# Delta rule's norms and gates inside attention's stage, GpSimd's level masks there too, and the modulation gates summed and spread in another way

## The chip, the cores and the metric

One core of one Trainium2 chip runs the whole kernel in one launch. The metric is the device time of that launch in microseconds (us), the median of several runs. TensorE multiplies matrices into PSUM, VectorE and ScalarE do element-wise work, GpSimd builds masks and does some element-wise work, and SyncE issues most of the transfers.

## What is computed

Two transformer layers over 256 tokens of width 1,024, in f32. The change lies in the first layer:

```python
mod = jax.nn.silu(c) @ w_ada + b_ada
shift1, scale1, gate1, shift2, scale2, gate2 = [m[:, None, :] for m in jnp.split(mod, 6, axis=-1)]
h = modulate(rms_norm(x, norm1_gain), shift1, scale1)
proj = h @ w_in
o_a = chunked_band_attention(qa, ka, va, attn_q_gain, attn_k_gain, attn_rel_bias)   # 8 heads of 64
o_a = rms_norm(o_a, attn_out_gain)
qkv_b = causal_depthwise_conv(qkv_b, dn_conv_w)
q_b = l2_norm(q_b); k_b = l2_norm(k_b)                                              # 4 heads of 128
beta = jax.nn.sigmoid(b_raw)
g = -jnp.exp(dn_a_log) * jax.nn.softplus(a_raw + dn_dt_bias)
o_b = gated_delta_rule(q_b, k_b, v_b, g, beta)                                      # chunks of 128
o_b = rms_norm(o_b, dn_out_gain) * jax.nn.silu(z_b)
x = x + gate1 * (jnp.concatenate([o_a, o_b], axis=-1) @ w_out)
h2 = modulate(rms_norm(x, norm2_gain), shift2, scale2)
x = x + gate2 * peer(h2, ...)
```

Within a chunk the delta rule needs the cumulated gates gc, the decays exp(gc_i - gc_j) below and above the diagonal, the Gram products k k^T and q k^T, and the inverse of a unit lower triangular matrix.

## The kernel before, in words

The program is a row of stages (`nc.Block`). At the end of each, all engines meet at a barrier. Within a stage each engine has its instructions in a fixed order, written out by hand, and waits on semaphores for the others. Nothing reorders them.

1. **First projection** (L637). c goes through SiLU and is kept as the same row on all 128 partitions (`c_row`). The first norm and the product with w_in run while the weights stream through a ring of four 1 MB slots. The modulation vector has 48 blocks of 128 outputs. Each takes one tile of w_ada, 128 x 1024, which VectorE multiplies with `c_row` and sums along the row (L752 for the first 16 tiles, `fill_mods` at L439 for the other 32). The tiles of `fill_mods` pass through five buffers, `fill_tiles`; `load_fills` (L430) lets SyncE load a tile once the sum before it in that buffer is done.
2. **Attention's stage** (L943). TensorE turns q and k (four banks), adds the bias and forms scores for two halves of four heads. VectorE takes the maxima (L970), ScalarE the exponentials (L1014), TensorE turns the probabilities in six banks, VectorE and ScalarE copy three each, TensorE forms the heads (L1079). Then come the row norm of the result (L989, L1026, L996) and, for the delta rule, the sums of squares of q and k as 16 products with one column (L1086). Between these, VectorE runs the last three taps of v's convolution (`add_tap`, L731) and nine tile sums. With gate 1's eight sums done, GpSimd stores the gate's column to HBM (`store_gate`, L447) and later loads it as a row on all partitions (`load_gate`, L453).
3. **Preparation of the delta rule** (L1122). VectorE spreads the inverse norms (L1178), TensorE turns them (L1239), VectorE scales q and k (L1200). The gate g is formed from a_raw by small operations on both engines, cumulated by TensorE (L1244), then come differences (L1206 to L1209), exponentials (L1166 to L1169), masks and beta (L1214 to L1217), the Gram products (L1251) and their scaling (L1221 to L1224), the transposes of k and v (L1255), and the scaled copies kbg, kdec and vb (L1231 to L1233). GpSimd writes six level masks meanwhile (`level_masks`, L1123).
4. **Inverse and delta rule** (L1275). Six doubling levels of 64 x 64 blocks: TensorE forms X (L1315), ScalarE copies it (L1365), TensorE forms the updates (L1320, L1321; all through `blocks`, L1301), VectorE subtracts them (L1395, L1397) and then does two tile sums. Products with u, w and the state, the output norm and the gating follow (L1412 to L1430).
5. **w_out** (`rows_stage`, L1433), the query stage (L1559), and the **experts' stage** (L1706), whose up half adds gate 2 times its result to x (L1972). Tile sums stand beside w_out's products and in the query stage; gate 2 goes through HBM like gate 1, at the start of the experts' stage (L1710).

The time of an f32 product lies in its passes: the profile counts two MATMUL rows for each. In the listings of the instructions one row stands for one product.

## Time and profile before

| | |
|---|---|
| Median of three runs | 1701.43 us (1698.95 to 1707.26) |
| The profiled execution | 1696.9 us, its span 1695.2 us, mean granted clock 0.973 |
| TensorE busy | 1582.3 us (93%) |
| VectorE busy | 1239.3 us (73%) |
| ScalarE busy | 899.9 us (53%) |
| GpSimd busy | 45.0 us (3%) |
| Moved by transfers | 314.37 MB, 185 GB/s on the mean |

Busy shares are means over very different stages, so a stage is read from its own window, and inside it from the order in time: which engine starts late, and who released it. The clock is the share of TensorE's 2.4 GHz that was granted; it stands at 1.0 or at 0.5 (1.2 GHz), and values between are stretches with a change inside.

### The profile page before, as it was taken

The numbers are of one execution on the slowest core, as the hardware profiler recorded it, in microseconds if no ns is written. First come the engines' busy times: TensorE is split into PE (matmuls) and PEld (weight loads), VectorE is DVE, ScalarE is ACT, GpSimd is POOL, SyncE is SP. The second block draws the span as 40 slices with busy tenths as digits, with TensorE's granted clock in tenths as the row PEclk, the third lists the DMA queues.
The fourth block names the chain that finished last, engine by engine and source line by source line (L and its number), as shares of the span: only waits on it lengthen the run. The fifth ranks groups of instructions, "written<-read, shape, count | busy, mean of one in ns | idle before, by whom it ended". The sixth has DMA issues, their size and how long they took to land. (4 is left out here: it accounts for less than half of the span.)

```text
span 1695.2 us, 26555 instructions
## 1 busy us (share of the span) xinstructions
PE 1582.3 (93%) x10358; PEld 1430.0 (84%) x10358; DVE 1239.3 (73%) x2494; ACT 899.9 (53%) x1497; POOL 45.0 (3%) x83
## 2 busy tenths in 40 slices
PE   5986779899999999999999999999999889889998
PEld 5975668899999999988888888797888777789997
DVE  5887777688997999957677666657787566654564
ACT  6763255555545555545555555456555756455453
POOL 0002300000000000000000000020000000000000
PEclk9997889999999999999999999989999899999999
DMA  9953446476666545557666666644444223345552
GB/s 325 342 173 103 151 168 195 119 238 229 227 224 212 162 149 163 153 205 252 238 244 239 246 239 238 243 143 157 144 140 139 75 75 123 132 151 191 176 195 102
DMA packets 110808, 314.37 MB, mean 185 GB/s; under 512 B 8464, under 2 KB 9056, under 8 KB 101216
## 3 DMA queue, kind: packets, MB, share of 16 engines
q1 hardware_dynamic: 98976, 276.94, 48.4%
q10 hardware_dynamic: 11040, 33.66, 5.5%
q0 software_dynamic: 672, 2.12, 0.4%
q8 instruction: 82, 1.34, 0.3%
q14 instruction: 38, 0.31, 0.1%
HBM read 293.80 MB, written 18.89 MB: 184 GB/s over the span
## 5 line engine op out<-in xcount | busy, mean ns | idle before, releaser
L300 PE MATMUL ps<-parts,parts 128*128 128x512 f32 (+1 forms) x4992 | 970.9, 356 | 20.9 <-DVE parts L290 15.1
L300 PEld LDWEIGHTS ps<-parts,parts 128*128 128x128 f32 x4992 | 823.4, 191 | 156.7 <-DVE parts L290 15.9
L285 ACT CAST parts<-lead 128x512 fp32r<-128x512 f32 x940 | 579.8, 621 | 618.2 <-PE ps L300 395.1
L290 DVE TENSOR_TENSOR parts<-lead,parts 128x512 fp32r<-128x512 f32 x940 | 640.7, 688 | 336.1 <-ACT parts L285 333.0
L1743 PE MATMUL ps<-parts,parts 128*128 128x256 f32 x3072 | 385.3, 285 | 4.5 <-DVE parts L290 4.5
L1743 PEld LDWEIGHTS ps<-parts,parts 128*128 128x128 f32 x3072 | 372.6, 192 | 5.5 <-DVE parts L290 5.5
L376 PE MATMUL ps<-lead,mem 128*128 128x128 f32 (+2 forms) x292 | 45.9, 321 | 51.0 <-ACT mem L492 26.4
L376 PEld LDWEIGHTS ps<-lead,mem 128*128 128x128 f32 (+2 forms) x292 | 40.3, 160 | 56.7 <-ACT mem L492 27.9
L1917 DVE TENSOR_SCALAR mem<-lead,mem 128x128 f32<-128x128 f32 x256 | 70.9, 338 | 0.0
L1729 PE MATMUL ps<-mem 128*128 128x128 f32 x512 | 67.8, 275 | 0.7 <-DVE mem L1917 0.7
L1729 PEld LDWEIGHTS ps<-mem 128*128 128x128 f32 x512 | 62.8, 192 | 1.1 <-issue 1.1
L1914 DVE TENSOR_SCALAR mem<-lead,mem 128x128 f32<-128x128 f32 x256 | 55.4, 278 | 0.0
L1947 DVE TENSOR_TENSOR mem<-mem 128x1024 f32<-128x1024 f32 x32 | 39.0, 1219 | 5.9 <-DMA mem<-act_spill 5.9
L1952 DVE TENSOR_TENSOR parts<-mem,parts 128x1024 fp32r<-128x1024 f32 x32 | 39.0, 1218 | 0.0
L1800 ACT CAST parts<-mem 128x1024 fp32r<-128x1024 f32 x32 | 33.4, 1045 | 9.1 <-DVE mem L1947 7.9
L1804 ACT COPY mem<-ps 128x512 f32<-128x512 f32 x64 | 37.0, 579 | 0.0
L1301 PE MATMUL ps<-mem 64*64 64x64 f32 x512 | 19.7, 238 | 17.7 <-POOL mem L1287 14.8
L444 DVE SCALAR_TENSOR_TENSOR mem<-mem 128x1024 f32<-128x1024 f32 x27 | 34.8, 1308 | 0.1
L1301 PEld LDWEIGHTS ps<-mem 64*64 64x64 f32 x512 | 18.3, 151 | 19.2 <-POOL mem L1287 16.1
L1783 ACT ACTIVATE mem<-ps 128x1024 f32<-128x1024 f32 x32 | 32.6, 1020 | 0.0
L2096 PEld LDWEIGHTS ps<-mem 128*128 128x128 f32 x256 | 29.8, 192 | 0.6
L2096 PE MATMUL ps<-mem 128*128 128x128 f32 x256 | 29.9, 275 | 0.0
(339 smaller groups left out, 972.8 us busy)
## 6 DMA issues: line engine op xcount, KB each, us to landing
...
act_spill<-mem ACTq DMA_DIRECT2D x32, 512.0 KB, 5.5
mem<-act_spill ACTq DMA_DIRECT2D x32, 512.0 KB, 3.3
mem<-in_w_ada SPq DMA_DIRECT2D x27, 512.0 KB, 5.3
...
```

The source lines that it names most:

```text
L285: act.copy(w_hi[g % BUFFERS], st.words(n, u * UNIT, UNIT)).then_inc(hi_ready, 1)
L290: dve.tensor_tensor(w_lo[g % BUFFERS], st.words(n, u * UNIT, UNIT), w_hi[g % BUFFERS].bitcast(F32), ALU.subtract).then_inc(lo_ready, 1)
L300: mm = pe.matmul(o, lhs[a], rhs[b], start=start and i == 0, stop=stop and i == 2, skip_group_check=True, **kw)
L376: last = pe.transpose(o, i, ident[0:i.shape[0], 0:i.shape[0]])
L1301: mm = pe.matmul(ps[rows, bank, u % 4 * HP:(u % 4 + 1) * HP], left[rows, :], right[rows, :], start=True, stop=True)
L1729: mm = pe.matmul(ps[:, 4 + b % 4, j * P:(j + 1) * P], one1[b % 2][:, j, :], one2[b % 2][:, j, :], start=True, stop=True)
L1743: mm = pe.matmul(ps[:, c % 2 * 2 + m // 2, m % 2 * S:(m % 2 + 1) * S], parts[a][:, ms], (x_hi, x_lo)[b][:, k, :], start=k == 0 and i == 0 ...
L1914: one = dve.tensor_scalar(one1[b % 2][:, j, :], iota, pick(0, b * GT + j), None, ALU.is_equal)
L1917: one = dve.tensor_scalar(one2[b % 2][:, j, :], iota, pick(1, b * GT + j), pick(2, b * GT + j), ALU.is_equal, ALU.mult)
L1947: dve.tensor_tensor(got[q % 2], got[q % 2], at(O_R + q * 1024, 1024), ALU.mult).then_inc(s_pr, 1)
L1952: dve.tensor_tensor(a_lo[q], got[q % 2], a_hi[q].bitcast(F32), ALU.subtract).then_inc(s_al, 1)
L2096: mm = pe.matmul(psf[:, 2048 + u * P:2048 + (u + 1) * P], k, q, start=True, stop=True)
```

## The change

- **Gate 1 on TensorE.** The eight tiles of gate 1 are stored on the host with the input index on partitions. c is turned in the first stage (eight transposes, one copy into `c_wide`, 64 equal columns for each of eight blocks). TensorE sums the gate over eight tiles as 16 products of 64 x 512, one half of the tile to PSUM partitions 0 to 63, the other to 64 to 127 of one bank (`gate_sums`), at the end of the preparation, behind the Grams. ScalarE copies the bank at that stage's end. At the end of the next stage four products with a single row of ones spread it (and its bias) over all partitions, and ScalarE copies it to `gate1`. Gate 1 no longer goes through HBM.
- **Order and buffers of the tiles.** Seven buffers instead of five. VectorE sums two tiles in attention's stage instead of nine, none instead of three in the preparation, eleven instead of thirteen in the inverse's stage, three instead of four beside w_out. Gate 2's eight tiles are loaded and summed in the up half, one every eight units (`load_late`, `late_mod`); its column is turned by TensorE before the store.
- **Moved to attention's stage:** the gate g and beta (beta by exp and reciprocal, not Sigmoid), the sums of squares of q and k (now four 512-column products with a matrix of ones, which give the sums spread over all partitions), their roots as exp(-0.5 ln), the scaling of q and k, the cumulated gates, and GpSimd's level masks. Scores lie in three banks per half instead of four, and VectorE copies all six banks of turned probabilities.
- **Preparation:** GpSimd masks the upper decay matrix with a select; ScalarE forms kbg and kdec from PSUM and does v's SiLU at the end. v is turned and scaled in the next stage.

```diff
-        FILL1, FILL2, FILL3, FILL4 = 9, 12, 25, 32
+        order = [KT, KT + 1] + list(range(KT)) + list(range(KT + 2, 3 * KT))
+        PE_SUMS = (2, KT + 2)
+        TAIL_SUMS = 21
...
+        def gate_sums(pe):
+            for p in range(*PE_SUMS):
+                k = order[p]
+                pe.wait_ge(s_fill[p % FILLS], 16 * (p // FILLS + 1))
+                for h in range(2):
+                    mm = pe.matmul(ps[h * 64:(h + 1) * 64, 7, :], c_wide[:, k, :],
+                                   fill_tiles[p % FILLS][:, h * 512:(h + 1) * 512], start=k == 0, stop=k == KT - 1)
+                mm.then_inc(s_mod, 1)
+        def load_late(sp, i):
+            sp.dma_start(late_tiles[i], A["w_ada"][(5 * KT + i) // 2][:, i % 2 * D:(i % 2 + 1) * D]).then_inc(s_late, 16)
...
@@ attention's stage, VectorE
+                dve.wait_ge(s_par_dn, 48)
+                step(dve.tensor_tensor(by_tile(gc_), ab[:, :, 1, :], dn_par[:, 4:8].unsqueeze(1).to_broadcast([P, TT, HD]), ALU.add))
+                step(dve.tensor_scalar(tmp_, gc_, -1.0, None, ALU.mult))
+                dve.tensor_tensor(tmp_, tmp_, gc_, ALU.max).then_inc(s_gpre, 1)
                 add_tap(dve, vstep, 2, 1)
-                fill_mods(dve, 0, 2)
+                fill_mods(dve, 0, PE_SUMS[0])
...
-                    fill_mods(dve, 2 + 2 * half, 4 + 2 * half)
-                for b in range(0, 6, 2):
+                for b in range(6):
...
+                for i in range(2):
+                    v = conv[:, 4 * i:4 * i + 4, :].rearrange("p a t -> p (a t)")
+                    dve.wait_ge(s_root, i + 1)
+                    dve.scalar_tensor_tensor(out=v, in0=v, scalar=1.0 if i else P ** -0.5, in1=qk_roots[:, i, :],
+                                             op0=ALU.mult, op1=ALU.mult)
+                dve.wait_ge(s_gcm, 1)
+                dve.tensor_copy(gcB, psf[:, 2560:3584].rearrange("p (u t) -> p u t", t=P))
@@ attention's stage, ScalarE, between and behind the exponentials
+                    if half == 0:
+                        act.wait_ge(s_silu, 1)
+                        act.activation(at(O_H, 8 * S), conv[:, 0:8, :].rearrange("p a t -> p (a t)"), ACT.Square).then_inc(s_sq, 1)
+                act.wait_ge(s_ge, 1)
+                act.activation(tmp_, tmp_, ACT.Ln, bias=1.0).then_inc(s_gl, 1)
+                for i in range(2):
+                    act.wait_ge(s_ssum, i + 1)
+                    act.activation(qk_roots[:, i, :], psf[:, 3072:4096], ACT.Ln, bias=eps).then_inc(s_ln, 1)
+                for i in range(2):
+                    act.wait_ge(s_ln, i + 1)
+                    act.activation(qk_roots[:, i, :], qk_roots[:, i, :], ACT.Exp, scale=-0.5).then_inc(s_root, 1)
@@ attention's stage, TensorE
+                    if b == 3:
+                        pe.wait_ge(s_sq, 1)
+                        square_sums(0)
...
+                    if hd == 4:
+                        pe.wait_ge(s_ln, 1)
+                        square_sums(1)
@@ preparation, GpSimd and ScalarE
-                level_masks(pool, lev, 6, s_lv, False)
+                pool.wait_ge(s_dexp, 2)
+                pool.affine_select(out=DT, in_=DT, compare_op=ALU.is_ge, fill=0.0, base=0, pattern=[[0, U], [1, P]],
+                                   channel_multiplier=-1).then_inc(s_upper, 1)
...
+                for u in range(U):
+                    act.activation(kbg[:, u, :], kt[:, u, :], ACT.Identity, scale=beg_[:, u:u + 1])
...
+                act.activation(conv[:, 8:12, :], conv[:, 8:12, :], ACT.Silu)
+                act.wait_ge(s_mod, PE_SUMS[1])
+                act.copy(gate_row, ps[:, 7, :])
@@ inverse, VectorE, per level, and TensorE at the end
-                    fill_mods(dve, FILL2 + 2 * i, FILL2 + 2 * i + 2)
+                    fill_mods(dve, PE_SUMS[1] + i, PE_SUMS[1] + i + 1)
...
+                fill_mods(dve, PE_SUMS[1] + 9, TAIL_SUMS)
                 dve.wait_ge(s_o, 1)
...
+                for h in range(2):
+                    pe.matmul(ps[:, h, :], ones[h * 64:h * 64 + 1, :], gate_row[h * 64:h * 64 + 1, :], start=True, stop=False)
+                for h in range(2):
+                    mm = pe.matmul(ps[:, h, :], ones[h * 64:h * 64 + 1, :], gate_bias[h * 64:h * 64 + 1, :], start=False, stop=True)
+                mm.then_inc(s_gb, 1)
@@ up half, SyncE and VectorE
+                st.issue(sp, n_up[0] + 24)
+                sp.wait_ge(s_pr, 12)
+                for i in range(KT):
+                    load_late(sp, i)
+                    st.issue(sp, n_up[0] + 26 + 2 * i)
...
+                    if i % 8 == 7 and 20 <= q < 20 + KT:
+                        late_mod(dve, q - 20)
```

How the instructions stand, at the two places of which the prediction speaks. First TensorE in the preparation, before (between the jumps of the two stages; L1239 spreads the norms, L1242 and L1244 cumulate the gates, L1251 are the Grams, L376 transposes):

```order
L1239 MATMUL ps<-lead,mem 128x128 x16
L1242 MATMUL ps<-mem,lead 128x8
L1244 MATMUL ps<-lead,mem 128x128 x8
L1251 MATMUL ps<-mem 128x128 x16
L376 MATMUL ps<-lead,mem 128x128 x16
```

and TensorE in the same stage of the changed kernel, with the first row of the next stage (L1300 are the Grams, L459 the sums of gate 1):

```order
L1300 MATMUL ps<-mem 128x128 x16
L376 MATMUL ps<-lead,mem 128x128 x8
L459 MATMUL ps<-mem 64x512 x8
L459 MATMUL ps<-lead,mem 64x512 x2
L459 MATMUL ps<-mem 64x512 x6
L1231 UNCONDITIONAL_BRANCH
L1343 UNCONDITIONAL_BRANCH
L376 MATMUL ps<-lead,mem 128x128 x8
```

The spreading of the norms and the cumulation went ahead into attention's stage, v's eight transposes behind the stage's end, and the sixteen products of the gate came in.

Second, VectorE from the start of attention's stage to the second maxima, before (L961 takes q and k out, L731 are taps, L444 tile sums, L970 the maxima):

```order
L961 TENSOR_SCALAR mem<-ps,lead 128x512 x2
L731 SCALAR_TENSOR_TENSOR mem<-mem,lead 128x256 x4
L444 SCALAR_TENSOR_TENSOR mem,lead<-mem 128x1024 x2
L970 TENSOR_REDUCE lead<-ps 128x4 x2
L974 TENSOR_SCALAR lead<-lead 128x2x4
L731 SCALAR_TENSOR_TENSOR mem<-mem,lead 128x256 x4
L444 SCALAR_TENSOR_TENSOR mem,lead<-mem 128x1024 x2
L970 TENSOR_REDUCE lead<-ps 128x4 x2
```

and in the changed kernel (L1033 takes q and k out, L1036 to L1038 the gate's sum, L765 taps, L449 tile sums, L1048 maxima):

```order
L1033 TENSOR_SCALAR mem<-ps,lead 128x512 x2
L1036 TENSOR_TENSOR lead<-mem,lead 128x8
L1037 TENSOR_SCALAR lead<-lead 128x8
L1038 TENSOR_TENSOR lead<-lead 128x8
L765 SCALAR_TENSOR_TENSOR mem<-mem,lead 128x256 x4
L449 SCALAR_TENSOR_TENSOR mem,lead<-mem,lead 128x1024 x2
L1048 TENSOR_REDUCE lead<-ps 128x4 x2
L1051 TENSOR_SCALAR lead<-lead 128x2x4
L765 SCALAR_TENSOR_TENSOR mem<-mem,lead 128x256 x4
L1048 TENSOR_REDUCE lead<-ps 128x4 x2
```

Three small operations stand ahead of the first tap, and the two tile sums between the maxima are gone.

## Rows read from the trace of the kernel before

**Rows 1.** Windows, whole kernel: stretch, us, then busy (instructions) of each engine, clock, DMA share, GB/s

```profile
107.50:141.20 33.70, 25.60 (x200) 24.06 (x200) 25.90 (x48) 20.01 (x50) 0.92 (x2) 0.87 0.51 159
141.20:172.10 30.90, 14.34 (x98) 13.91 (x98) 24.92 (x39) 10.99 (x15) 10.40 (x25) 0.72 0.21 68
172.10:214.80 42.70, 31.49 (x608) 29.34 (x608) 31.41 (x69) 11.13 (x35) 13.76 (x8) 0.86 0.46 150
...
760.00:1085.00 325.00, 324.76 (x1432) 268.43 (x1432) 229.89 (x302) 174.48 (x271) 0.00 (x0) 1.00 0.69 245
```

**Rows 2.** DMA issues by line: KB each, median us from issue to landing

```profile
mem<-in_w_ada SPq DMA_DIRECT2D x27, 512.0 KB, 5.3
...
lead<-in_dn_out_gain SPq DMA_DIRECT2D x1, 64.0 KB, 4.3
...
gate_rows<-lead POOLq DMA_DIRECT2D x2, 4.0 KB, 10.3
```

**Rows 3.** Order in time, attention's stage: start us, duration us, engine, line, operation

```profile
108.34 0.43 SPq L948 DMA_DIRECT2D lead<-in_dn_out_gain  x1
...
109.73 1.66 DVE L731 SCALAR_TENSOR_TENSOR mem<-mem,lead 128x256 f32<-128x256 f32 x4
...
113.80 1.82 DVE L970 TENSOR_REDUCE lead<-ps 128x4 f32<-128x512 f32 x2
...
115.86 0.37 ACT L1014 ACTIVATE mem<-ps,lead 128x128 f32<-128x128 f32 x1 [0.21 <-DVE lead L974]
...
121.78 0.37 ACT L1014 ACTIVATE mem<-ps,lead 128x128 f32<-128x128 f32 x1 [2.60 <-DVE lead L974]
...
124.96 1.95 ACT L1018 ACTIVATE mem<-mem 128x2048 f32<-128x2048 f32 x1
...
127.53 6.20 PE L1079 MATMUL ps<-mem 128*128 128x64 f32 x48
...
136.58 1.28 ACT L1029 ACT_TABLE_LOAD   x1
137.87 0.29 ACT L1029 ACTIVATE lead<-lead 128x2 f32<-128x2 f32 x1
...
138.40 1.54 DVE L996 SCALAR_TENSOR_TENSOR mem<-mem,lead 128x512 f32<-128x512 f32 x2
```

**Rows 4.** Order in time, preparation of the delta rule: TensorE, GpSimd, VectorE

```profile
143.25 6.75 PE L1239 MATMUL ps<-lead,mem 128*128 128x128 f32 x32 [4.74 <-DVE mem L1178]
...
151.36 0.51 POOL L1148 COPY mem<-mem 64x384 f32<-64x384 f32 x1
...
153.02 3.84 PE L1251 MATMUL ps<-mem 128*128 128x128 f32 x32 [1.01 <-DVE mem L1200]
...
159.90 1.22 DVE L1214 TENSOR_TENSOR mem<-mem,lead 128x1024 f32<-128x1024 f32 x1 [1.54 <-ACT mem L1169]
...
170.17 1.21 DVE L1233 TENSOR_TENSOR mem<-ps,mem 128x1024 f32<-128x1024 f32 x1
```

**Rows 5.** Order in time, inverse and delta rule

```profile
180.67 0.28 DVE L1395 TENSOR_TENSOR mem<-mem,ps 128x128 f32<-128x128 f32 x1
...
185.68 3.12 PEld L1301 LDWEIGHTS ps<-mem 64*64 64x64 f32 x96 [1.31 <-issue]
...
195.62 0.28 DVE L1395 TENSOR_TENSOR mem<-mem,ps 128x128 f32<-128x128 f32 x1
...
196.60 1.14 PE L1325 MATMUL ps<-mem 64*64 64x64 f32 x16 [0.59 <-DVE mem L1397]
...
206.85 0.69 DVE L1417 COPY mem<-ps 128x512 f32<-128x512 f32 x1 [1.62 <-PE ps L1344]
```

**Rows 6.** Windows of TensorE alone: stretch, us, busy (instructions), clock, DMA share, GB/s

```profile
145.00:147.50 2.50, 2.50 (x14) 0.50 0.55 120
...
177.50:180.00 2.50, 2.50 (x48) 0.50 0.17 49
...
215.00:217.50 2.50, 2.50 (x13) 0.50 0.00 0
```

444 lines of the change are left out of this document (233 added, 211 removed).

## Prediction, made before the changed kernel was run

> **What bounds the kernel now.** I read the windows of each stage first, then the waits and the order in time inside the three stages that the change rewrites, and last the landing times of the transfers. The windows [rows 1] show four of the stretches: attention's stage 107.5 to 141.2 us, the preparation of the delta rule 141.2 to 172.1, the inverse and the delta rule 172.1 to 214.8, and the up half of the experts' stage. Behind the third TensorE is busy nearly all the time (324.8 of 325.0 us in the up half), so only added waits could be felt there. In the first three no engine is full: 25.6, 14.3 and 31.5 us of TensorE, 25.9, 24.9 and 31.4 of VectorE. They are chains of small steps that hand work from engine to engine, with a barrier at each end. The preparation is the thinnest: 30.9 us, mostly one VectorE chain, which ends with six multiplications between 160 and 171.4 [rows 4] while TensorE does nothing.
>
> **Attention's stage: longer by 5.0.** (1) VectorE now computes the gate's sum behind its first two evacuations, and that waits for all three delta parameters. The last of them is issued at 108.34 [rows 3] and lands 4.3 later [rows 2], at 112.6. The gate's three small operations take about 0.8, so the first tap begins at 113.5, where it began at 109.73 [rows 3]. The two gate-tile sums behind it stay, so the first maximum starts at 117.6, not 113.80, and the first exponentials at 119.7, not 115.86. (2) Each half of the exponentials takes 3.3 [rows 3]. ScalarE's square of 1.95 moves between the halves. The second half so ends at 119.7 + 3.3 + 1.95 + 3.3 = 128.3; it ended when the square began, at 124.96: + 3.3. VectorE is not late for it, since the two gate-tile sums of 1.2 between the maxima are gone. (3) From there to the last head was 8.7 us (to 127.53 + 6.20 [rows 3]). Now TensorE adds the second pair of sums of squares between the heads. They are two 512-column products in f32; 128 columns cost 3.84 / 32 = 0.12 a pass [rows 4], two passes each, so four times that comes to 1.9 for both. VectorE copies all six transposed banks; three take 1.9 and are early. The heads end at 138.5, which is 4.8 later. (4) Behind the heads stood 6.2 us, to the end of the last row at 138.40 + 1.54 [rows 3]. Now: two evacuations 1.3, two normalisations of q and k of 1.22, the copy of the cumulated gates 1.2, small ones 0.4, the two rows 1.5, in sum 6.8. The stage ends at 145.3 and the barrier's 1.2 follow: 146.2 to 146.5 against 141.2, so **+5.0** (3 to 8: three if the parameters land after 2.5 us as the earlier two did, eight if TensorE, idle for 4.7 us before the transposes, runs them and the heads at half clock). Hidden there: GpSimd's masks, 10.7 us from the stage's start to 151.9 [rows 4], which nothing needs before the inverse.
>
> ScalarE's table changes in this stage go from three to five. A change costs 1.28 in the rows, and the next operation starts 0.01 behind it (136.58 + 1.28, then 137.87 [rows 3]). The two new ones run beside TensorE's heads, so I cost them at nothing; without that cover they cost 2.6. The Trainium skill, "ScalarE: Activation LUTs", What ACT_TABLE_LOAD costs, puts a drain of about 1.38 us to each change, some 2.66 in all. By that this stage would be 2.8 longer still. The trace disagrees, since its rows leave no room for a drain.
>
> **The preparation: shorter by 12.7.** Spreading of norms, gates, cumulated sums and the scalings of k and v leave VectorE. Its new chain is ten operations of 0.7 to 1.2 and two short waits, about 12 us, with GpSimd's select (128 x 64 elements take 0.3 to 1.5, so 128 x 1024 about 2) beside it. ScalarE's chain, with 12 scalings of about 0.3, two table changes and the SiLU of v, ends near 14. The longest is now TensorE's, because the gate's eight sums are queued behind the Grams, and ScalarE waits for them at the stage's end. Its terms from the start: 16 Gram products at the clock that TensorE has after idling, 6.8 (the first 32 passes of this stage took 6.75 with 0.50 granted [rows 4, 6]); 8 transposes 1.0; then 16 products of 64 x 512, 32 passes of 4 x 0.12 less their tails, 14.4 us if one runs after the other. But the two halves of a tile go to different column halves of the array. For such pairs the nearest rows are the 64 x 64 blocks of the inverse, which differ in rows and columns: 96 passes in 3.12, 0.033 each, where unpaired ones need 1.14 / 16 = 0.071 [rows 5]. That is an overlap by two or more; a pair that shares its rows may do less. I take a factor of 1.6: 8.9 us, between 7.2 and 14.4. With ScalarE's copy of 0.6, the barrier's 0.7 and 0.2 of hand-over: 6.8 + 1.0 + 8.9 + 1.5 = 18.2 against 30.9, so **-12.7** (-14.4 to -7.2). The last gate tile is loaded once the first sum is done and lands 5.3 later [rows 2], about 14 us in, before its turn. The bias is fetched by 1,024 elements of 4 bytes, as the store of the gate was, which took 10.3 [rows 2]; it is wanted only in the next stage.
>
> The Trainium skill, "TensorE: Matmul & The Clock Gate", Why this matters for your kernels, says that products with few output columns overlap if each goes to its own column group, 2.38 times for three of them. By that two halves would come close to full overlap, 7.5 us, and the sum would be 1.4 lower. No row of the trace before has such a pair.
>
> **Inverse and w_out: shorter by 4.1.** VectorE's gate-tile sums go from two to one per level. The updates begin at 180.67 and then every 3.7 us on the mean until 195.62 [rows 5]. TensorE alone needs 3.1 a level for its 96 passes plus a hand-over, 3.3, so four intervals give 1.6 back. The first level runs at half clock now (0.50 until 180 us). Behind the sums TensorE is warm, and with one sum less the second update comes 2.4 earlier. The scaling of v by ScalarE (0.7 a level) and its transposes (1.0) fit into waits. At the end two sums stand between the copies and the first output rows, which are ready at 206.85 [rows 5]: +0.5; the broadcast of the gate by four products and two ScalarE copies ends 0.1 behind the old end: +0.6 in all. It also keeps TensorE busy up to w_out's transposes, which now run at 0.50 [rows 6]: -0.7. Sum: -1.6 - 2.4 + 0.6 - 0.7 = **-4.1** (-6 to -1).
>
> **Elsewhere: nothing.** In the first stage the transposes and the copy of c fall into VectorE's and TensorE's waits before 21 us. The last eight tiles are loaded and summed in the up half: 1.3 us of VectorE every 10.9, where it is idle 95 of 325 us [rows 1], and 47 GB/s on top of 245 with the transfer engines busy 0.69. If that cover is gone, a stall of 1 us per tile costs 8.
>
> **Sum.** +5.0 - 12.7 - 4.1 = -11.8. The profiled execution took 1696.9 us, so 1685.1. The median of the runs stands 4.5 above it, at 1701.4; I add half of that and predict **1687.5**.
>
> **Rivals.** *The halves don't overlap.* The preparation is then only 7.2 shorter, the sum -6.3, the time 1693. For it: they read the same rows and no row shows such a pair; against it: the 64 x 64 pairs do overlap. *Attention's stage grows by 10* (half clock, the roots on the path): -6.8, 1692.5. For it: the clock was 0.50 in the preparation [rows 6] after 4.7 us without work [rows 4], and the new gaps are about as long. *The sums bind the stage and slow the kernel:* if TensorE stays at half clock through the preparation and the halves don't overlap, the sums take 28.8, the stage 6.8 + 2 + 28.8 + 1.5 = 39, which is 8 longer; with +5.0 and about -3 behind it: +10, 1709. It decides once the sums take longer than 24 us. For it: in the inverse TensorE stayed at 0.50 for 6 us of work; against it: 512-column products keep it far busier, and it reached full clock within 7 us in each stage. *It doesn't do what it says:* the masks were done at 151.9 [rows 4] while the stage lasted to 172, so moving them is worth nothing by itself; that is in my sum already.
>
> **How the numbers follow.** A run of this kernel tells 0.5% (8.5 us) from no change. Forecast (-8.5 to -18) 0.60; no overlap 0.18; long attention 0.12; the sums at half clock 0.07; 0.03 for full overlap and everything hidden, below the range. The range takes the forecast's bounds, the two middle cases and part of the last: 1679 to 1700. Faster 0.63, same 0.30, slower 0.07.
>
> **What would show it.** Right: the preparation lasts about 18 us and its last wait is ScalarE's for the gate's sums, which run in 8 to 10 us; attention's stage lasts 38 to 39 with the first maximum near 117.6; TensorE is at full clock at the inverse's first level and at w_out's start; the up half stays at 325. Wrong: sums of 14 us or more, a first maximum near 114, or new waits for transfers in the up half.

## The result, and the profile after

The changed kernel ran in a median of **1680.01 us** (1679.39 to 1681.05, four runs) against 1700.38 us before (1698.95 to 1707.26, four runs): a ratio of 0.9873, 95% interval 0.9856 to 0.9889. It is faster by 20.4 us, or 1.1 to 1.4%: under 2%, but clear of the noise, since the interval leaves out 1. Its profiled execution took 1681.05 us, with a span of 1679.3 us, so span against span the change gives 15.9 us. I had predicted 1685.1 for the profiled execution and 1687.5 for the median: the right direction, inside the range of 1679 to 1700, and too slow by 7.5 us. The 15.9 lies within the forecast's own bounds (8.5 to 18 less), the medians' 20.4 beyond them.

First the windows of the changed kernel, cut at its own stage starts, with the up half last (columns as in [rows 1]):

```profile
107.74:142.93 35.19, 27.18 (x194) 23.32 (x194) 25.08 (x49) 25.36 (x55) 9.73 (x23) 0.92 0.16 48
142.93:157.66 14.73, 13.77 (x73) 8.77 (x73) 10.54 (x14) 10.24 (x21) 1.64 (x2) 0.85 0.39 115
157.66:198.50 40.84, 31.81 (x624) 28.51 (x625) 27.66 (x62) 14.19 (x45) 11.96 (x8) 0.96 0.46 154
744.00:1069.00 325.00, 324.96 (x1435) 268.65 (x1434) 238.94 (x320) 174.84 (x270) 1.15 (x2) 1.00 0.75 258
```

With the stage starts of the kernel before read to the hundredth (107.53, 141.17, 172.06, 214.88), the stages compare so (the 0.7 us that the prediction gave to w_out's start falls into the row below the inverse's):

| us | before | predicted | after | step was off by |
|---|---|---|---|---|
| attention's stage | 33.64 | +5.0 | 35.19 (+1.6) | -3.4 |
| preparation | 30.89 | -12.7 | 14.73 (-16.2) | -3.5 |
| inverse's stage, w_out | 42.82 | -4.1 | 40.84 (-2.0) | +2.1 |
| all else, up half included | | 0 | +0.7 | +0.7 |
| sum | | -11.8 | -15.9 | -4.1 |

A stage's start is here the first operation of any engine behind the barrier. Before the change that was GpSimd's at 172.06, 0.4 us behind the barrier; cut at the barrier's end, the preparation gave 15.8 and the inverse 2.4.

The windows of the up half were both chosen 325 us long, so they compare its rate and not its length: TensorE is busy for 324.96 us with 1,435 rows of products, against 1,432 before [rows 1], with VectorE 9 us busier and the transfers at 0.75 instead of 0.69. VectorE waits there for transfers (of `act_spill`) five times, 3.4 us in all, against once and 0.2 before. These are the new waits that the prediction named as a sign of being wrong, but TensorE doesn't feel them. With all behind the inverse at 1480.8 us against 1480.3, the cover held.

**Attention's stage** of the changed kernel, order in time (the rows that answer to [rows 3]):

```profile
112.64 0.17 DVE L1036 TENSOR_TENSOR lead<-mem,lead 128x8 f32<-128x8 f32 x1 [2.60 <-DMA lead<-in_dn_out_gain]
...
113.16 1.68 DVE L765 SCALAR_TENSOR_TENSOR mem<-mem,lead 128x256 f32<-128x256 f32 x4
...
117.20 1.81 DVE L1048 TENSOR_REDUCE lead<-ps 128x4 f32<-128x512 f32 x2
...
122.43 1.95 ACT L1114 ACTIVATE mem<-mem 128x2048 f32<-128x2048 f32 x1
...
127.64 1.53 PE L376 MATMUL ps<-lead,mem 128*128 128x128 f32 x12
...
129.01 2.79 PE L1201 MATMUL ps<-mem 128*128 128x64 f32 x24
...
131.64 1.94 PE L1167 MATMUL ps<-mem,lead 128*128 128x512 f32 x4
...
133.41 2.79 PE L1201 MATMUL ps<-mem 128*128 128x64 f32 x24
...
136.31 1.29 DVE L1071 TENSOR_TENSOR mem<-ps,lead 128x512 f32<-128x512 f32 x2 [4.26 <-PE ps L1201]
...
141.25 1.41 DVE L1085 SCALAR_TENSOR_TENSOR mem<-mem,lead 128x512 f32<-128x512 f32 x2
```

The predicted wait is there: VectorE stands 2.60 us for the last of the parameters, and the first maximum starts at 117.20 (predicted 117.6). The heads take 2 x 2.79 = 5.6 us where they took 6.2, and the last row ends at 142.66, only 0.27 ahead of the next stage.

**The preparation** of the changed kernel, order in time (against [rows 4]):

```profile
142.97 5.87 PE L1300 MATMUL ps<-mem 128*128 128x128 f32 x32 [4.71 <-PEq L1011]
...
147.89 1.12 POOL L1245 TENSOR_SCALAR_AFFINE_SELECT mem<-mem 128x1024 f32<-128x1024 f32 x1 [4.45 <-ACT mem L1254]
...
149.64 3.65 PE L459 MATMUL ps<-mem 128*64 128x512 f32 x16
...
153.13 1.03 PE L459 MATMUL ps<-lead,mem 128*64 128x512 f32 x4
...
153.55 1.22 DVE L1292 TENSOR_TENSOR mem<-ps,mem 128x1024 f32<-128x1024 f32 x1
...
153.99 2.74 PE L459 MATMUL ps<-mem 128*64 128x512 f32 x12
...
156.78 0.58 ACT L1266 COPY mem<-ps 128x512 f32<-128x512 f32 x1 [1.47 <-PE ps L459]
...
157.66 1.06 PE L376 MATMUL ps<-lead,mem 128*128 128x128 f32 x8 [0.93 <-PEq L1231]
```

As predicted the stage ends in ScalarE's wait for the gate's sums. These take 7.1 us (149.64 to 156.73), not 8.9. VectorE is done at 154.77.

**The inverse**, order in time (against [rows 5]), and TensorE's windows alone (against [rows 6]):

```profile
164.06 0.28 DVE L1463 TENSOR_TENSOR mem<-mem,ps 128x128 f32<-128x128 f32 x1
...
166.79 4.32 PE L1349 MATMUL ps<-mem 64*64 64x64 f32 x128 [0.35 <-issue]
...
172.64 7.06 PE L1349 MATMUL ps<-mem 64*64 64x64 f32 x211 [1.52 <-issue]
...
178.81 0.29 DVE L1463 TENSOR_TENSOR mem<-mem,ps 128x128 f32<-128x128 f32 x1 [0.57 <-PE ps L1349]
...
198.50 3.59 PE L376 MATMUL ps<-lead,mem 128*128 128x128 f32 x16 [2.38 <-PEq L1323]
```

```profile
145.00:147.50 2.50, 2.50 (x15) 0.54 0.20 1
...
185.00:187.50 2.50, 2.50 (x14) 0.50 0.41 164
...
200.00:202.50 2.50, 2.50 (x14) 0.62 0.00 0
```

The second update starts 6.40 us after the stage's start (164.06 - 157.66) where it started 8.61 after it (180.67 - 172.06). But the next four intervals take 14.75 us, hardly less than the 14.95 before: in the third, at the fourth level, TensorE stands for 1.52 us with no releaser ("issue"). At the start of w_out the clock is again at half (0.50 from 198.5 to 201.9).

### The profile page after: what moved, and what is told of

It is laid out like the page before. It is cut to its first block and busy times, and to the rows that moved or that the text cites. A ratio compares the mean times of both kernels' runs of the same rounds, so it can differ in the third digit from the quotient of the medians.

```text
span 1679.3 us, 26490 instructions
## 1 busy us (share of the span) xinstructions
PE 1586.3 (94%) x10351; PEld 1426.4 (85%) x10351; DVE 1226.5 (73%) x2476; ACT 907.7 (54%) x1519; POOL 42.7 (3%) x82
## 5 line engine op out<-in xcount | busy, mean ns | idle before, releaser
L376 PE MATMUL ps<-lead,mem 128*128 128x128 f32 (+2 forms) x292 | 45.5, 319 | 44.9 <-ACT mem L519 23.4
L376 PEld LDWEIGHTS ps<-lead,mem 128*128 128x128 f32 (+2 forms) x292 | 39.8, 159 | 52.6 <-ACT mem L519 24.8
L786 DVE SCALAR_TENSOR_TENSOR lead<-lead 128x1024 f32<-128x1024 f32 x16 | 18.9, 1218 | 2.1 <-DMA lead<-in_w_ada 2.1
```

The source lines that it names most:

```text
L376: last = pe.transpose(o, i, ident[0:i.shape[0], 0:i.shape[0]])
```

## Experiments

Fifteen more runs were made, one of them the changed kernel unedited. What each left in its profiled execution is gathered here (us). Most were executed once, so the verdicts rest on the stages and not on the times. The changed kernel's own two rows show how far a stage moves with no edit at all: 1.7 us in attention's stage, 0.4 in the preparation, 1.0 in the inverse.

| kernel | whole | attention | preparation | inverse | all behind it | TensorE's waits for "issue" in the inverse |
|---|---|---|---|---|---|---|
| before | 1696.9 | 33.64 | 30.89 | 42.82 | 1480.3 | 0.37 |
| square between (before) | 1696.8 | 33.96 | 30.90 | 42.27 | 1480.2 | none |
| store later (before) | 1700.6 | 32.84 | 30.94 | 46.00 | 1480.4 | none so named |
| changed | 1681.1 | 35.19 | 14.73 | 40.84 | 1480.8 | 0.35, 1.52 |
| changed, again | 1682.8 | 36.89 | 15.13 | 39.89 | 1481.6 | 0.65, 1.25 |
| same columns | 1694.1 | 36.58 | 21.85 | 39.04 | 1486.9 | none |
| no sums | 1681.2 | 36.54 | 13.32 | 42.09 | 1480.8 | none |
| gate later | 1678.1 | 32.79 | 14.98 | 39.85 | 1482.3 | 0.37, 1.52 |
| parts early | 1679.2 | 35.25 | 14.33 | 40.03 | 1480.3 | 1.06, 0.15 |
| both | 1684.5 | 32.95 | 15.74 | 39.50 | 1486.8 | 1.25, 0.37 |
| scaling in preparation | 1687.2 | 36.06 | 17.14 | 43.70 | 1480.8 | 0.47, 1.52 |
| masks in preparation | 1690.7 | 36.61 | 15.18 | 42.05 | 1487.4 | 0.32, 1.24 |
| upper on VectorE | 1679.9 | 36.33 | 15.03 | 40.63 | 1478.2 | 0.46, 1.52 |
| short loads | 1681.1 | 35.21 | 14.08 | 39.65 | 1481.3 | none |
| short loads, two sums | 1684.1 | 35.61 | 14.13 | 43.48 | 1481.4 | none |
| loads held | 1686.7 | 36.60 | 15.00 | 39.11 | 1485.7 | none |
| gate later, loads held | 1680.0 | 32.72 | 15.55 | 39.67 | 1482.6 | 0.21 |

The spread of attention's stage goes with TensorE's clock. In the three kernels with the gate later the granted clock is 1.00 from 115 to 137 us, and the stage lasts 32.7 to 33.0. In the other versions of the changed kernel it falls to 0.50 around the first transposes of the probabilities: for 3.4 us where the stage lasts 35.2 to 36.1 (the changed kernel's first profile, from 123.4 to 126.8), for 6.8 where it lasts 36.3 to 36.9 (its second, from 122.3 to 129.1).

### Do the column halves overlap?

```diff
-                    mm = pe.matmul(ps[h * 64:(h + 1) * 64, 7, :], c_wide[:, k, :],
+                    mm = pe.matmul(ps[0:64, 7 - h, :], c_wide[:, k, :],
```

> The changed kernel, with both halves of each gate tile sent to the same 64 output columns of TensorE (PSUM partitions 0 to 63 of two banks). The second half of gate 1 is therefore not the reference's. In the changed kernel the 32 passes take 7.1 us and the preparation lasts 14.7. Theory: this is so because the two halves run beside each other, and the sums are what the preparation ends with. Then the sums take 14.2 us here (32 x 0.44), the preparation 21.8, and the time is about 7 us longer, 1688. Rival: a pass with 64 output columns is simply short (0.22 us), whatever its neighbour does. Then the sums stay at 7.1 us and the preparation at 14.7.

Order in time of TensorE, of this kernel:

```profile
151.54 7.08 PE L459 MATMUL ps<-mem 128*64 128x512 f32 x16
158.46 1.88 PE L459 MATMUL ps<-lead,mem 128*64 128x512 f32 x4
160.18 5.31 PE L459 MATMUL ps<-mem 128*64 128x512 f32 x12
```

The 32 passes take 13.95 us (151.54 to 165.49) instead of 7.1, and the preparation 21.85 instead of 14.73. The expectation came true in both places, and the overlap is a factor of 1.97, practically full. The time rose by 13 us, not by 7. The other 6 lie behind the inverse (1486.9 against 1480.8) and come again in kernels whose results are the reference's (both, masks in preparation), so nothing ties them to this edit. About 5 of the 6 can be placed: in all three of these kernels the granted clock is 0.50 for 10.2 us near 1380 (1385.1 to 1395.3 here) with TensorE busy throughout, where the changed kernel has 1.00; half of that time is 5.1.

### What bounds the preparation next, and does TensorE stay warm?

```diff
-                    mm = pe.matmul(ps[h * 64:(h + 1) * 64, 7, :], c_wide[:, k, :],
-                                   fill_tiles[p % FILLS][:, h * 512:(h + 1) * 512], ...)
+                    mm = pe.matmul(ps[h * 64:(h + 1) * 64, 7, 0:8], c_wide[:, k, :],
+                                   fill_tiles[p % FILLS][:, h * 512:h * 512 + 8], ...)
```

> The changed kernel with each of the gate's products cut from 512 to 8 columns, so that gate 1 is not computed and TensorE does nearly nothing behind the transposes of the preparation. Theory: the sums hide all but their last 1.4 us behind ScalarE's chain, so the preparation ends with ScalarE's SiLU of v and lasts 13.2 us instead of 14.7; and, as my prediction priced it, they keep TensorE warm, so that without them the first level of the inverse runs at half clock and the inverse's stage is about 2.4 us longer than 40.8. Rival: the inverse's first level is bound by GpSimd's and VectorE's hand-overs, not by the clock; then the preparation is 1.5 shorter and the inverse stays within 0.5 us of 40.8.

The preparation lasts 13.32 us and ends, as expected, behind ScalarE's SiLU of v, which has no wait behind it any more. So sums worth 7.1 us cost 1.4. The inverse is 1.25 us longer than the changed kernel's although it has no stop. Its second update starts 8.63 us after the stage's start (6.40 there): 2.2 us, close to the 2.4 that the prediction gave to the warm clock and one sum less together. The granted clock, which with the sums is 1.00 from 147.3 to 184.8, is 0.50 here from 154.8 to 165.1. The four intervals behind it take 12.56 us.

### ScalarE's square between the halves

```diff
 @@ before: attention's stage, ScalarE
                     one.then_inc(s_exp, 1)
+                    if half == 0:
+                        act.wait_ge(s_silu, 1)
+                        act.activation(at(O_H, 8 * S), ..., ACT.Square).then_inc(s_sq, 1)
-                act.wait_ge(s_silu, 1)
-                act.activation(at(O_H, 8 * S), ..., ACT.Square).then_inc(s_sq, 1)
                 for b in range(1, 6, 2):
```

> The kernel before, with ScalarE's Square of 1.95 us moved from behind the second half of the exponentials to between the halves; all else as before. My prediction added the full 1.95 us to attention's stage for this move. By that pricing the stage goes from 33.7 us to 35.6. Rival: in the kernel before the square stood ahead of ScalarE's three copies of the turned probabilities, and the heads waited for those; moved, it costs 1.95 in one place and gives it back in the other, and the stage stays at 33.7 within 0.4.

Order in time of ScalarE and TensorE, of this kernel:

```profile
119.20 1.95 ACT L1019 ACTIVATE mem<-mem 128x2048 f32<-128x2048 f32 x1
...
121.94 0.37 ACT L1014 ACTIVATE mem<-ps,lead 128x128 f32<-128x128 f32 x1 [0.80 <-DVE lead L974]
...
125.33 2.66 PE L376 MATMUL ps<-lead,mem 128*128 128x128 f32 x12 [4.40 <-ACT mem L1014]
...
127.78 6.03 PE L1080 MATMUL ps<-mem 128*128 128x64 f32 x48
```

The stage is 0.3 us longer, so the result is the rival's, but its reason is not. The second half of the exponentials starts when it did, at 14.3 us from the stage's start, because ScalarE had waited 2.60 us there for the second maxima [rows 3]. The square fills that wait and leaves 0.80 of it. A gap is worth as much as the work that is put into it. In the changed kernel this wait is gone, as the two tile sums between the maxima are, and ScalarE goes through the first half, the square and the second half without a stop (119.25 to 127.59). There the square does cost its 1.95, as the prediction had it.

### Who holds the barrier of attention's stage?

```diff
 @@ before, GpSimd: attention's stage, preparation
-                store_gate(pool, 0, 2)
+                pass
...
+                store_gate(pool, 0, 2)
                 level_masks(pool, lev, 6, s_lv, False)
```

> The kernel before, with GpSimd's store of gate 1 to HBM moved from attention's stage to the start of the preparation; all else as before. The last VectorE row of attention's stage ended at 139.94 us and the next stage began at 141.17, which is 1.23 later; in the changed kernel the gap is 0.27. Theory: GpSimd reaches the barrier only when its store of 10.3 us has landed (issued 130.66, so 140.96), and this sets the end of the stage. Then the gap is 0.3 here and attention's stage is 0.9 shorter, 32.8 us, while the preparation stays at 30.9. Rival: the gap is the barrier's own cost; then it stays at 1.2 and nothing changes.

VectorE at the stage's end, of this kernel:

```profile
139.55 1.54 DVE L996 SCALAR_TENSOR_TENSOR mem<-mem,lead 128x512 f32<-128x512 f32 x2
141.63 0.25 DVE L1177 RECIPROCAL lead<-lead 128x16 f32<-128x16 f32 x1 [0.54 <-PEq L943]
```

The gap is 0.54 us where it was 1.26, and attention's stage 32.84 where it was 33.64. GpSimd's store, which takes 10.3 us to land [rows 2], held the barrier: before, it landed at 140.85 and GpSimd reached the barrier at 140.97. The time as a whole doesn't show the gain. In this one execution the inverse took 46.00 us instead of 42.82, with a tile sum beside GpSimd of 2.33 instead of 1.31 and the clock at 0.50 once more from 187.9 to 191.3. The change removes it with gate 1's way through HBM. I had carried the 1.2 over as the barrier's own cost.

### The parameters' wait

```diff
 @@ changed kernel: attention's stage, VectorE (the three small operations with their wait)
-                dve.wait_ge(s_par_dn, 48) ... .then_inc(s_gpre, 1)
                 add_tap(dve, vstep, 2, 1)
-                fill_mods(dve, 0, PE_SUMS[0])
+                fill_mods(dve, 0, 1)
+                dve.wait_ge(s_par_dn, 48) ... .then_inc(s_gpre, 1)
+                fill_mods(dve, 1, PE_SUMS[0])
```

> The changed kernel, with the gate's three small VectorE operations (which wait for the delta rule's parameters) moved from ahead of v's tap to between the two tile sums; nothing left out. Attention's stage lasted 35.2 us in the changed kernel's profile and 36.5 in two of its variants that changed nothing there; VectorE waited 2.6 to 3.2 us for the parameters, and where it waited longer TensorE turned the first probabilities in 2.8 us, not 2.1. Theory: the wait is on the stage's path, so the first maximum comes at 7.0 us from the stage's start and not at 9.5, and the stage lasts 32 to 33 us. Rival: behind the wait something else is late (TensorE's products, ScalarE's two SiLUs, which end 8.7 us from the start), and no more than 1 us is gained.

VectorE and TensorE, of this kernel, whose stage starts at 106.48:

```profile
111.89 0.17 DVE L1038 TENSOR_TENSOR lead<-mem,lead 128x8 f32<-128x8 f32 x1 [0.27 <-DMA lead<-in_dn_out_gain]
...
113.53 1.81 DVE L1049 TENSOR_REDUCE lead<-ps 128x4 f32<-128x512 f32 x2
```

```profile
118.97 1.53 PE L376 MATMUL ps<-lead,mem 128*128 128x128 f32 x12 [0.88 <-ACT mem L1110]
```

The first maximum comes 7.05 us from the start, and the stage lasts 32.79 us. That is 2.4 below the changed kernel's profile and 4.1 below its second one. The second part is the clock: where VectorE comes late, TensorE has been idle for 4.05 us and turns the first probabilities at half clock, 2.82 us against 1.53 above. This row is of the changed kernel run again:

```profile
123.14 2.82 PE L376 MATMUL ps<-lead,mem 128*128 128x128 f32 x12 [4.05 <-ACT mem L1109]
```

### Scalings and masks, back in the preparation

```diff
 @@ preparation, VectorE and TensorE (and out of attention's stage)
+                for i in range(2):
+                    ... dve.scalar_tensor_tensor(out=v, in0=v, ..., in1=qk_roots[:, i, :]).then_inc(s_qkn, 1)
+                pe.wait_ge(s_qkn, 2)
```

> The changed kernel, with VectorE's two scalings of q and k by their inverse norms (2.35 us) moved back to the start of the preparation, the Grams waiting for them; nothing left out. Theory: in attention's stage they stand beside ScalarE's squares, table load and root for the row norm, so taking them out gives back 1.0 to 1.2 us of it, while the preparation becomes longer by the full 2.4 us, since the Grams and the sums behind them are its path: +1.3 in sum, 17.1 us for the preparation. By my prediction's pricing (all 2.4 us on attention's path, and the preparation bound by TensorE) the two cancel and the sum is 0. Third possibility: TensorE, idle for longer ahead of the Grams, stays at half clock for longer, and the preparation is more than 3 us longer.

```profile
137.25 1.29 DVE L1071 TENSOR_TENSOR mem<-ps,lead 128x512 f32<-128x512 f32 x2 [4.26 <-PE ps L1196]
...
141.66 0.29 ACT L1124 ACTIVATE lead<-lead 128x2 f32<-128x2 f32 x1
```

The preparation is longer by 2.4 us against the changed kernel's profile and by 2.0 against its second one, about the 2.35 of the scalings. In attention's stage the way from VectorE's first evacuation of the heads to the next stage is 6.62 us (137.25 to 143.87), and it is 6.62 in the changed kernel too (136.31 to 142.93). The move gives nothing back there. ScalarE's roots, squares, table load and square root bind that end, and VectorE's scalings lie beside them. ScalarE's squares could start when VectorE's evacuations end at 137.60 in the changed kernel, and they start at 137.95, when the roots are done; so the roots and their table change cost 0.35 us there and not nothing. My theory's gain of 1.0 to 1.2 was wrong, and so was the prediction, which had put VectorE's 6.8 us on the path and found nearly the right length with the wrong engine. The inverse of this execution, 43.70, has the stop of 1.52 again and then the clock at 0.50 from 177.9 to 181.3, which the changed kernel doesn't have.

```diff
 @@ GpSimd: level masks out of attention's stage, ahead of the select in the preparation
-                pool.wait_ge(s_tr, 4)
-                level_masks(pool, lev, 6, s_lv, False)
...
+                level_masks(pool, lev, 6, s_lv, False)
                 pool.memset(TI_all[HP:P, :, 0:HP], 0.0).then_inc(s_zero, 1)
```

> The changed kernel, with GpSimd's level masks (10.7 us) moved back to the start of the preparation, ahead of its select of the upper decay matrix; nothing left out. Theory: in attention's stage nothing waits for the masks, and in the preparation they delay the select to about 153.7 us and VectorE's last product to about 156, still before TensorE's sums end at 156.7: both stages stay as they are, within 0.3 us. Rival: GpSimd's masks beside VectorE's chain slow it (in the inverse a tile sum beside GpSimd took 2.08 us, not 1.22), so that VectorE ends behind TensorE and the preparation is 1 to 3 us longer, while attention's stage, freed of the masks, is shorter by up to 1 us.

```profile
155.73 1.34 POOL L1245 TENSOR_SCALAR_AFFINE_SELECT mem<-mem 128x1024 f32<-128x1024 f32 x1
...
156.04 1.31 DVE L1288 COPY mem<-mem 128x512 f32<-128x512 f32 x1
...
157.98 1.23 DVE L1292 TENSOR_TENSOR mem<-ps,mem 128x1024 f32<-128x1024 f32 x1
```

The preparation is 15.18 us (15.13 and 15.00 in two executions with the masks in attention's stage), so the masks' place is worth nothing that can be told. It is close, though. The select comes 11.4 us after the stage's start, the copy of 0.43 us takes 1.31 beside it, and VectorE's last product ends 0.3 ahead of the next stage, together with ScalarE's copy. With the masks here, TensorE and VectorE bind the stage alike. Attention's stage did not gain by their absence (36.61).

```diff
 @@ preparation: select on GpSimd -> product on VectorE
-                pool.affine_select(out=DT, in_=DT, ...).then_inc(s_upper, 1)
+                dve.tensor_tensor(DT, DT, upper.unsqueeze(1).to_broadcast([P, U, P]), ALU.mult).then_inc(s_upper, 1)
```

> The changed kernel, with the upper decay matrix masked by a VectorE product with the 0/1 matrix (1.22 us), as in the kernel before, and not by GpSimd's select; nothing left out. Theory: VectorE ended at 154.8 us in the changed kernel, 1.9 ahead of TensorE's sums at 156.7, so 1.2 more still lie beside them and the preparation stays at 14.7 us within 0.3. Rival: in that case the wait for the select was VectorE's own slack, and with the product inside its chain the first parts of L come later; then the preparation is still the same but VectorE ends less than 1 us ahead. It would be worth 1 us or more only if VectorE were the bound.

The preparation lasts 15.03 us, inside the spread of the unedited one, and the time is 1679.91. VectorE ends at 156.52, 1.7 us ahead of TensorE's sums. The GpSimd select is worth nothing here while these end the stage.

### The inverse: VectorE's sums, GpSimd's parts, TensorE's stop

> The changed kernel, with 32 of the 1,024 columns of each of the last fourteen tiles of w_ada loaded in the preparation and the inverse (the same number of transfers, 16 KB each for 512 KB), so that shift and scale 2 are not the reference's. In the inverse of the changed kernel TensorE stood still for 1.5 us after no semaphore at 171.1, while one 16 KB packet of its instructions had arrived at 170 behind tile transfers that filled the queues; the kernel before had such an interval too, and in two variants of the changed kernel the five levels took 3.14 us each without it. Theory: TensorE's instructions come late behind the tiles. Then there is no such stop here, the updates follow each other every 3.1 us and the inverse lasts 38.7 us instead of 40.8. Rival: the stop has nothing to do with the tiles and comes in about every second execution; then this run shows it or not, and the level intervals that contain an instruction packet are long as well.

```diff
+                wide_ = D if p < PE_SUMS[1] else 32
-                sp.dma_start(fill_tiles[p % FILLS], A["w_ada"][j][:, half * D:(half + 1) * D])
+                sp.dma_start(fill_tiles[p % FILLS][:, 0:wide_], A["w_ada"][j][:, half * D:half * D + wide_])
```

TensorE in the levels, of this kernel, which is one unbroken row of 15.14 us:

```profile
162.98 15.14 PE L1350 MATMUL ps<-mem 64*64 64x64 f32 x464 [0.50 <-DVE mem L1466]
```

The stop is gone, and the second to sixth updates start at 164.86, 167.82, 170.96, 174.09 and 177.23, so 12.37 us for four intervals instead of 14.75. The inverse lasts 39.65 us, not 38.7. From the last first-half update to w_out it takes 20.9 us against 19.7, with the clock lower there. That end differs by up to 2.5 us between executions of all versions.

> The changed kernel, with SyncE's last seven tile loads held until VectorE has summed the tile of the fifth level; nothing left out. In the changed kernel they start at 163 us, and TensorE stops at 171.1 for 1.5 us. With short loads (one thirty-second of the bytes) the stop was gone and the levels took 3.14 us each. Theory: it is the tile bytes that keep TensorE's instructions waiting; held back, they leave the fourth level free, the five updates follow each other every 3.1 us, and the inverse is 1.5 to 2.2 us shorter than 40.8, unless the sums at its end now wait for their tiles. Rival: the short loads removed the stop through the tiles loaded in the preparation, not through these seven; then it stays.

```diff
+                sp.wait_ge(s_mod, PE_SUMS[1] + 5)
                 load_fills(sp, PE_SUMS[1] + FILLS, 3 * KT)
```

```profile
164.68 11.51 PE L1350 MATMUL ps<-mem 64*64 64x64 f32 x350 [0.50 <-DVE mem L1466]
```

With all results kept, holding back seven tiles removes the stop as well: four intervals take 12.46 us, and the inverse 39.11 (39.89 in the changed kernel beside it). The changed kernel's second execution shows the stop once more, at the same level (1.25 us). So it follows from the tile transfers, and not from the last seven alone: it is absent too in same columns, where the first two of these seven are issued at the same times from the stage's start (6.5 and 8.8 us), but the eight tiles before them over 12.0 us instead of 6.0 (150.76 to 156.77 in the changed kernel).

That it is TensorE's instructions which come late behind them shows in where the stops stand. Count the MATMUL rows of the whole kernel, starting with 0. The nine executions with such waits have 17 of them in the inverse, and each stands just ahead of row 978 (979 in parts early and both), row 1106 or row 1234. These are 128 rows apart, whatever the level and whatever the engines beside TensorE do; the x128 between the waits of 0.35 and 1.52 above is one such stretch. The instructions arrive in packets of 16 KB, about one for each stretch. In the six executions with the long stop ahead of row 1106, the packet that precedes it begins 3.3 to 3.6 us after row 978 has started; in same columns, no sums, short loads, held loads and the last version below, which have no stop there, it begins 0.6 to 1.6 us after it. At every one of the 17 stops TensorE goes on 1.25 to 1.51 us after a packet has ended: in the changed kernel the packet ends at 171.38 and row 1106 starts at 172.64. So the instructions come late, and with the tile loads taken away they don't; the queue in which the packets wait isn't seen.

> The kernel with the short loads, and with two tile sums behind each level of the inverse (as before the change) instead of one, and none further on in that stage; shift and scale 2 are not the reference's. My prediction priced the second sum at 0.4 us a level (1.6 for four intervals). By that the interval between updates is 3.5 to 3.7 us here. Rival: TensorE's 96 products and two hand-overs make the interval, a second sum of 1.15 us fits behind the updates, and the interval is 3.1 to 3.3 us, so that what the change saved in the levels was not VectorE's sums.

```diff
 @@ short loads, and
-                    fill_mods(dve, PE_SUMS[1] + i, PE_SUMS[1] + i + 1)
+                    fill_mods(dve, PE_SUMS[1] + 2 * i, min(PE_SUMS[1] + 2 * i + 2, TAIL_SUMS))
```

Without a stop, and with two sums a level, the four intervals take 14.51 us (166.06 to 180.57), 3.63 each against 3.09, and the second update starts 2.2 us later (8.60 after the stage's start). On the mean the prediction's 0.4 a level holds, with 0.5. But that is in part luck: the first interval alone takes 4.43 against 2.96, with a tile sum of 2.28 beside GpSimd, and the other three take 3.36 on the mean against 3.14. The 8.60 also says what the warm clock is worth by itself. With warm clock and two sums the second update starts at 8.60, with cold clock and one sum (no sums) at 8.63, with both unfavourable (before) at 8.61, or 9.0 counted from the barrier, and only with both favourable at 6.40. Each of the two holds the first level back by itself, and removing one of them gives 0.4 at most.

> The changed kernel, with GpSimd's first three level parts (L times mask, 1.58 us each) formed in the preparation behind its select, not at the start of the inverse; nothing left out. In the inverse of the changed kernel VectorE's first update of T took 0.59 and 1.16 us and its first tile sum 2.08 instead of 1.22 while GpSimd worked, and TensorE waited 0.6 us twice for GpSimd's parts. Theory: these hand-overs and the slowing of VectorE beside GpSimd are on the path of the first level, so its second update starts 4.9 us after the stage's start instead of 6.4 and the inverse is about 1.5 us shorter, while the preparation stays at 14.7, because TensorE's sums end it. Rival: GpSimd beside VectorE in the preparation slows VectorE's last operations past TensorE's end, and what the inverse gains the preparation loses.

```diff
 @@ preparation, GpSimd, behind the select (and out of the inverse)
+                pool.wait_ge(s_L, 1)
+                for i in range(3):
+                    pool.tensor_tensor(Cm[i], L, lev[:, i:i + 1, 0:HP].to_broadcast([P, U, HP]), ALU.mult)
```

VectorE in the preparation's last part and TensorE in the levels, of this kernel:

```profile
152.40 1.50 DVE L1291 COPY mem<-mem 128x512 f32<-128x512 f32 x1
153.82 1.76 DVE L1293 TENSOR_TENSOR lead<-lead,mem 128x512 f32<-128x512 f32 x1
155.62 1.23 DVE L1295 TENSOR_TENSOR mem<-ps,mem 128x1024 f32<-128x1024 f32 x1
...
165.47 8.74 PE L1352 MATMUL ps<-mem 64*64 64x64 f32 x255 [1.06 <-issue]
174.37 2.87 PE L1352 MATMUL ps<-mem 64*64 64x64 f32 x83 [0.15 <-issue]
```

The second update comes 4.64 us after the stage's start, so 1.8 earlier than in the changed kernel, but a stop of 1.06 us falls into the first interval behind it, and the inverse is 0.8 us shorter than in the changed kernel's first profile and no shorter than in its second (39.89). GpSimd slows VectorE's two operations by 1.07 us each, yet VectorE ends (156.85) 0.3 ahead of the next stage, and the preparation is no longer for it.

### Versions that put the gains together

> The changed kernel with two of the edits tried one at a time: the gate's three small operations behind v's tap (attention's stage 32.8 us instead of 35.2 to 36.5), and GpSimd's first three level parts in the preparation (the first level's second update 4.6 us after the stage's start instead of 6.4); nothing left out. Theory: the gains lie in different stages and add: 2.4 to 3.7 in attention's stage, 1.2 to 1.8 behind it, so 4 to 5 us below the changed kernel, a median near 1675.5. Rival: what varies from one execution to the next (TensorE's idle time that follows no semaphore in the inverse, late weights behind it) is as large, so that the median shows under 2 us of it.

This kernel holds the edits of the gate later and the parts early. The stage gain in attention is there (32.95), and the median is not: 1681.97 us (1675.14 to 1684.53, six runs), ratio 0.988, interval 0.9855 to 0.9905. The profiled execution, the slowest of the six, lost 1.0 us in the preparation and 6.0 behind the inverse. The first isn't the work of GpSimd's parts: the clock came up 6.0 us after the preparation's start instead of 4.4, and it did so too in the last version below, which hasn't that edit and whose preparation took 15.55. The expected 1675.5 is missed by 6.5 us, which is more than the edits were worth.

> The changed kernel once more, unedited, beside the two versions of this set on the same chip, to learn how far its stages and its median vary. If the stop of TensorE in the inverse follows from the tile transfers, it is here again, about 1.5 us long at the fourth level; attention's stage lasts 35.2 or about 36.5 us; the median lies between 1679 and 1683 us. If the stop comes by chance, it may be missing or stand at another level.

> The changed kernel with the gate's three small operations behind v's tap and the last seven tile loads held; nothing left out. Theory: 2.4 to 3.7 us less in attention's stage and 1.5 to 2.2 less in the inverse make 4 to 6 us, and as neither touches the preparation, where the version with both earlier edits was 1 us longer, the median is 4 to 5 us below that of the changed kernel run beside it. Rival: the half-clock stretches behind the inverse, which differ by up to 6 us between executions of all versions, take most of it, and the two medians differ by less than 2 us.

The changed kernel's second set met its expectation: the stop at the fourth level, 36.89 us in attention's stage, a median of 1682.76.

The last version is the edit of the gate later with that of the held loads. On one chip, in one set: the changed kernel again 1682.76 us (1679.77 to 1686.17, five runs; ratio 0.9897, interval 0.9878 to 0.9916), the version with the gate later and the loads held 1677.91 us (1676.92 to 1679.98, four runs; ratio 0.9867, interval 0.9849 to 0.9885). It is 4.8 us below the changed kernel there, as expected, and 2.1 below the changed kernel's first median. The two intervals of this set overlap by a little, so its lead of some 2 to 5 us is likely and not certain. The two profiled executions differ by 2.8 us, and not where the theory put it: 4.2 less in attention's stage, but 0.4 more in the preparation, 0.2 less in the inverse (1.5 to 2.2 expected) and 0.9 more behind it. Its stop has shrunk to 0.21 us and the four intervals take 13.02 us instead of 14.81, yet what follows them takes 1.6 us longer. That holding the loads adds anything to the time isn't shown: the gate later alone took 1678.07 in its one execution, the loads held alone 1686.71.

## Why the prediction was too slow

Three terms of the sum failed. Step (3) of attention's stage carried a stretch over that held half-clock work; the factor of 1.6 for the two column halves was 1.97; and the inverse's levels left out TensorE's stop behind the tile loads, which went the other way. So the stages are off by -3.4, -3.5 and +2.1, and the last hides part of the first two. Almost half of the whole miss comes from none of them but from the offset between a profiled execution and a median.

**Attention's stage, +5.0 predicted, +1.6 in the profile (up to +3.3 in others).** Step (1) holds: the wait for the parameters puts the first maximum at 9.46 us from the start (predicted 10.1). Step (2) holds: the square and both halves end at 19.85 (predicted 20.8). Step (3) failed. I kept the 8.7 us from the last exponential to the last head and added 1.9 for the second pair of sums; it took 8.6 in all. (The two make 10.6; the text has the heads end at 138.5, 10.2 behind the exponentials, so it lost 0.4 on the way, and then 0.3 more between 145.3 + 1.2 and the 146.2 behind the +5.0. Added up as written, the step is +5.3 to +5.7, and was off by more.) The 8.7 contained half-clock work. Before, the clock was 0.50 from 125.5 to 128.9, and the second transposes took

```profile
125.16 2.55 PE L376 MATMUL ps<-lead,mem 128*128 128x128 f32 x12 [4.40 <-ACT mem L1014]
```

where they take 1.53 now, and the heads 6.2 and 5.6. The first pair of sums runs up to the moment when the second exponentials end (124.56 to 127.59), so that TensorE has no gap of 4.40 us there, and the clock is back at 1.00 at 126.8, before the transposes. That it is these sums which bring it back is argued from this order; no run leaves them out. Step (3) is 1.6 of the 3.4. Behind the last row the sum had 0.9 and it took 0.3: another 0.6, and the store moved alone shows 0.8 of it. The first maximum (0.6), the exponentials (0.3) and the tail (0.3) make up the rest. Masks and scalings cost nothing in this stage, as predicted for the masks; the scalings are hidden by ScalarE, which the prediction had not seen. The next operation starts 0.01 to 0.02 us behind each of the new table changes (127.61 + 1.28, then 128.90; 134.74 + 1.28, then 136.04), so a change costs 1.28 to 1.30, and the prediction was right to count no more; the cover it gave them was 0.35 short.

**The preparation, -12.7 predicted, -16.2 measured.** The path was right (Grams, transposes, sums, ScalarE's copy, barrier), and so was its last wait. The mis-sized term is the sums: 8.9 with a factor of 1.6, measured 7.1 with a factor of 1.97 (shown by the same columns), which is 1.8 of the 3.5. Then 1.1 for the Grams, priced at half clock throughout at 6.8, while the clock comes up at 147 and they take 5.87; and 0.6 for the end, where 1.5 were given for copy, barrier and hand-over and 0.93 were needed. The Trainium skill, "TensorE: Matmul & The Clock Gate", Why this matters for your kernels, has products in different column groups overlap 2.38 times for three of them. The runs agree that such products overlap, and the pair here, two f32 halves of 512 columns that share their rows, comes nearer to its full factor: 1.97 of 2. The prediction took 7.5 us from that rule and then chose 8.9 for want of a row; the 7.5 would have been the better estimate. Full overlap was the case to which it gave 0.03.

**The inverse and w_out, -4.1 predicted, -2.0 measured.** The first level gave 2.2 (predicted 2.4); the runs without sums and with two sums a level each give it back, so it takes TensorE's warm clock and one sum less together. The levels gave 0.2 instead of 1.6. Without the stop they would have given 2.5 (12.4 against 14.95, short and held loads). TensorE's stop behind the tile transfers took most of it: 1.52 us in the third interval and 0.35 in the first; another 0.2 lies in the second, where a tile sum beside GpSimd took 2.09 instead of 1.22. The stop was not in the prediction in any form, and the tile loads that the preparation's sums release within 6 us are part of the change. The end cost 0.4 (predicted 0.6). The 0.7 at w_out did not come: the gate's four products end 2.38 us ahead of that stage, TensorE stands, and the clock is 0.50 from the stage's start at 198.5 to 201.9.

**The offset.** I added half of the 4.5 us between the median and the profiled execution of the kernel before. That execution (1696.9) was a fast one: in five sets the kernel before took, on the median, 1697.98 to 1703.88 (two of the sets have one execution of it). The profiled execution of the changed kernel stands 1.0 above its own median, so this term alone is 3.4 of the 7.5 us. Half of the difference was a guess, and no run bears it out. The changed kernel's second set gave 1682.8. Read over both sets the gain is 17.5 to 20.4 us.

Of the signs that the prediction named, these came: the last wait of the preparation, the first maximum near 117.6, full clock at the inverse's first level, an up half at its old rate. These did not: a preparation of 18 us (14.7), sums of 8 to 10 (7.1), attention's stage of 38 to 39 (35.2 and 36.9), full clock at w_out. Of the signs of being wrong one came, the new waits for transfers in the up half (3.4 us of VectorE), at no cost.

None of the rivals occurred: the halves overlap, attention's stage grew by less, not more, and the sums run at full clock. The masks' move is worth nothing by itself, as was said, and neither is the select.
